# High and low parts of each row block side by side in SBUF, and FFN up chunks 1 to 3 and 23 in the wide two-part product

## The chip, the cores and the metric

The kernel runs on one core of one Trainium2 chip. The metric is device time in microseconds (us) of one execution; lower is better. Before the change the median of 3 runs is 851.08 us (850.93 to 851.29).

## What is computed

The reference chains two transformer-like blocks over 256 tokens of width 1024. Only one part of the first block matters here, its feed-forward network:

```python
h = rmsnorm(x, ffn_pre_norm[l])
up = causal_dwconv(h @ w_ffn_up[l], ffn_conv_w[l], ffn_conv_b[l])   # 1024 -> 6144, 3 taps over tokens
f_gate, f_val = jnp.split(up, 2, axis=-1)
f = (jax.nn.gelu(f_gate, approximate=True) * f_val) @ w_ffn_down[l] # 3072 -> 1024
x = x + rmsnorm(f, ffn_post_norm[l])
```

Everything is float32. The kernel reaches that precision on TensorE by splitting each operand into a high part, which TensorE takes in one pass (type fp32r), and a low part, the rest. A product is then three matmuls: high by high, weights high by rows low, and weights low by rows high.

## The kernel before

**Weights.** They come in as 258 units of 128 x 1024. For each unit SyncE starts a transfer, ScalarE copies it to the high part (L1359), VectorE subtracts to get the low part (L1942), and TensorE uses both. Four places hold split units, so ScalarE can split a unit only when TensorE is done with the unit four before it. The program of each engine is written out by hand; an engine works through its own list strictly in order, and semaphores tie the lists together.

**Rows.** The activations (8 blocks k of 128 channels by 256 tokens) are held as a high and a low part too: tile `HX` with views `Hh` and `Hl`, and tile `BR` with views `YBh` and `YBl`. In both, all eight high blocks stand first and all eight low blocks behind them.

**FFN up.** There are 24 chunks, fu0 to fu23, each of two units (one gives the gate channels, one the value channels). Per unit and block k there are two ways:

- `chunk` with `three`: three matmuls of 256 columns (L666, L667, L668), all summed in one half of a PSUM bank. Chunks fu1, fu2, fu3 and fu23 go this way; fu0 too, in another order (`chunk_by_k`).
- `chunk_apart` with `apart` (L719): the high weights meet high and low rows in one matmul of 512 columns, and the low weights meet the high rows in one of 256 columns, which is added to the second half of the bank. Each unit has a bank of its own, and VectorE sums the two halves with one reduction a unit (L2665) into `FSUM`. The list `APART` (L259), here fu4 to fu22, says which chunks go this way.

After a chunk come, in this order: (for `APART` the two reductions on VectorE), the convolution's first tap on ScalarE (two instructions, L1370), its other taps on VectorE (four instructions, L1963), gelu on ScalarE, the product of gate and value on VectorE (L1953), its high part on ScalarE (into `YBh`), its low part on GpSimd (L2757; for fu23 on VectorE). On VectorE the splits of two coming units and the product of the chunk before stand ahead of a chunk's reductions or taps.

**FFN down.** After each odd chunk from fu3 to fu21, two units of `fd` multiply finished products: `down_rows`, 12 matmuls a unit, 512 columns of weights moving past a stationary row block. The last four units stand behind fu23 in an order of (token half, unit) written out by hand, in which the product of chunk 23 (i = 3) comes fifth, as `(0, 3)`. Behind that follows `second_norm`, the norm of the sum over all chunks on ScalarE and VectorE, beside TensorE's memory values (mk2, mk3); the second block's first products (`vu`) need its result.

Two more lines are touched: unit `SPARE` (153) is split into `BR` while that is free, and `bank_table` gives each chunk its banks (for odd chunks in `APART` banks 2 and 0, for even ones 1 and 3).

Of the kernel before, what the change touches and what calls it, by code (L numbers as in the profile page):

```python
# [8 lines left out]
R = mybir.dt.float32r  # L9
# [7 lines left out]
P = 128  # L17
T = 256
# [237 lines left out]
    return {"g": name[:5], "u": name[:5], "w": name.split("_")[0], "m": "mv", "v": name[:2]}[name[0]]  # L256


APART = [f"fu{j}" for j in range(4, 23)]  # L259
SPARE = FIRST["mk2"] + 1  # L260


def place(q):

    return (q - (q > SPARE)) % NS
# [9 lines left out]
def bank_table():  # L275

    bank, n = {}, 1
    for name, _, _ in STREAM:
# [8 lines left out]
        elif name in ("mk0", "mk1"):  # L287
            bank[name] = 1 + int(name[2])
        elif name[:2] == "fu" and name in APART:
            for i in range(2):  # L290
# [66 lines left out]
def build_program(nc, first, gates, ws, par, con, masks, bd, rows, swt, xin, xtok, min_, post, decay, gates2, out):  # L357
    ctx = ExitStack()
    with ctx:
        def sb(name, shape, dt=F):  # L360
            return ctx.enter_context(nc.sbuf_tensor("t_" + name, shape, dt))
# [10 lines left out]
        PB = [ctx.enter_context(nc.psum_tensor(f"bank{i}", [P, 512], F)) for i in range(8)]  # L372
# [18 lines left out]
        BR = sb("br", [P, 2, 2048], R)  # L391

        def ar(kb, *shape):
            n = 1
            for k in shape:
                n *= k
            v = ARENA[:, kb * 256:kb * 256 + n]
            if len(shape) == 2:
                return v.rearrange("p (a b) -> p a b", a=shape[0])
            if len(shape) == 3:  # L400
                return v.rearrange("p (a b c) -> p a b c", a=shape[0], b=shape[1])
            return v
# [3 lines left out]
        WL = [sb(f"wl{i}", [P, 1024], R) for i in range(NS)]  # L406
# [3 lines left out]
            return BR[:, 0, 0:1024] if q == SPARE else WH[place(q)][:, :]  # L410

        def low(q):
            return BR[:, 1, 0:1024] if q == SPARE else WL[place(q)][:, :]

        HX = sb("hx", [P, 2, 8, T], R)
        Hh, Hl = HX[:, 0, :, :], HX[:, 1, :, :]
        SM = sb("sm", [P, 394])
        NW = SM[:, 304:352].rearrange("p (a b) -> p a b", a=3)
        NW2 = SM[:, 352:364].rearrange("p (a b) -> p a b", a=3)
# [26 lines left out]
        DTS = WH[NS - 1][:, 0:256].rearrange("p (k c) -> p k c", k=8)  # L446
        BAW = ar(60, 8, 8)
        BAS = BR[:, 0, 0:128].rearrange("p (k c) -> p k c", k=8)
        YBh, YBl = (BR[:, i, :].rearrange("p (k t) -> p k t", k=8) for i in range(2))
        MEMF, MEMQ = ar(16, 8, T), ar(24, 8, T)  # L450
        MG = ar(36, 8, T)
        MP = ar(44, 8, T)
# [47 lines left out]
        def half(bank, j):  # L500
            return PB[bank][:, T * j:T * j + T]

        def two(bank):
            return PB[bank][:, :].rearrange("p (k t) -> p k t", k=2)

        def ffn_source(name, i):

            return FSUM[:, 2 * (int(name[2:]) % 2) + i, :] if name in APART else half(BANK[name], i)

# [152 lines left out]
        def pe_program(e):  # L662
# [7 lines left out]
            def mm(o, l, r, st=True, sp=True):  # L670
                return e.matmul(o, l, r, start=st, stop=sp, skip_group_check=True)  # L671
# [4 lines left out]
            def weights(q, a):  # L676
                return [w.rearrange("p (a b) -> p a b", a=a) for w in (high(q), low(q))]
# [40 lines left out]

            def apart(b, wh, wl, k):  # L719

                mm(two(b), wh[:, k, :], HX[:, :, k, :], k == 0, False)
                return mm(half(b, 1), wl[:, k, :], Hh[:, k, :], False, k == 7)

            def chunk_apart(name):
                for j in range(2):
                    q = walk.unit()
                    wh, wl = weights(q, 8)
                    split_ready(q)
                    bank_free((name, j))
                    for k in range(8):  # L730
                        if k == 4:
                            walk.mid()
                        m = apart(BANK[name, j], wh, wl, k)
                    m.then_inc(*unit.now(q))
                    walk.tick()

            def chunk_by_k(name, xh, xl, x_ready):
                b = BANK[name]
                qs = [walk.unit(NS - 1 - j) for j in range(LAST[name] - FIRST[name] + 1)]
                for q in qs:  # L740
                    split_ready(q)
                bank_free(name)
                for k in range(8):
                    x_ready(k)
                    for j, q in enumerate(qs):
                        wh, wl = weights(q, 8)
                        m = three(half(b, j), wh[:, k, :], wl[:, k, :], xh[:, k, :], xl[:, k, :], k == 0 and j == 0, k == 7)
                        if k == 7:
                            m.then_inc(*unit.now(q))
# [421 lines left out]
            def normed(tag):  # L1171
                def ready(k):
                    e.wait_ge(*(g_hl if k % 2 and tag == "mix" else d_hl).of(tag, k))
                return ready
# [80 lines left out]
            for j in range(24):  # L1255
                if j == 0:
                    chunk_by_k("fu0", Hh, Hl, normed("fpre"))
                elif f"fu{j}" in APART:
                    chunk_apart(f"fu{j}")
# [94 lines left out]
        def act_program(e):  # L1354
# [441 lines left out]
            for j in range(24):  # L1796
                name = f"fu{j}"
                walk.cols(name, j == 0)
                e.wait_ge(*(d_ev.of(name) if name in APART else unit.of(LAST[name])))
                if j >= 2:  # L1800
# [138 lines left out]
        def dve_program(e):  # L1939
            def split(q):  # L1940
                e.wait_ge(*hi.of(q))
                e.tensor_tensor(low(q), RAW[q % NR][:, :], high(q).bitcast(F), SUB).then_inc(*lo.now(q))  # L1942
# [716 lines left out]
            for j in range(24):  # L2659
                name = f"fu{j}"  # L2660
                walk.cols(name, j == 0)
                if name in APART:
                    for i in range(2):
# [310 lines left out]
```

## Time and profile before

| what | value |
|---|---|
| median of 3 runs | 851.08 us (850.93 to 851.29) |
| profiled execution: span | 849.0 us |
| median less span (start and end around the profiled instructions) | 2.1 us |
| TensorE matmul busy | 836.9 us (99%) |
| VectorE busy | 650.2 us (77%) |
| ScalarE busy | 508.5 us (60%) |

The profiled execution's own time is not listed apart from its span; the 2.1 us are the median less the span. A matmul's row gives its start and its whole length through the array, and matmuls overlap in it, so what a matmul costs in a stream is the distance from its start to the next one's start, called its pitch here. The same holds, more weakly, for VectorE, where an instruction's last stretch overlaps the next.

### The profile page before, as it was taken

The numbers are of one execution on the slowest core, as the hardware profiler recorded it, in microseconds if no ns is written. First come the engines' busy times: TensorE is split into PE (matmuls) and PEld (weight loads), VectorE is DVE, ScalarE is ACT, GpSimd is POOL, SyncE is SP. The second block draws the span as 40 slices with busy tenths as digits, with TensorE's granted clock in tenths as the row PEclk, the third lists the DMA queues.
The fourth block names the chain that finished last, engine by engine and source line by source line (L and its number), as shares of the span: only waits on it lengthen the run. The fifth ranks groups of instructions, "written<-read, shape, count | busy, mean of one in ns | idle before, by whom it ended". The sixth has DMA issues, their size and how long they took to land. (4 is left out here: it accounts for less than half of the span.)

```text
span 849.0 us, 13946 instructions
## 1 busy us (share of the span) xinstructions
PE 836.9 (99%) x5422; PEld 755.0 (89%) x5422; DVE 650.2 (77%) x1171; ACT 508.5 (60%) x840; POOL 76.1 (9%) x76
## 2 busy tenths in 40 slices
PE   8999999999999999999999999999999999999996
PEld 7999999999989988888888799899899888888885
DVE  6887987998877877888777868778855566776764
ACT  6575778665377755565657878754553454545443
POOL 0100002001020211111111200140000020000000
PEclk9999999999999999999999999999999999999999
DMA  8657443467455655546555454644423332455541
GB/s 314 236 170 279 152 147 125 148 200 296 148 178 189 220 186 200 181 167 213 184 188 185 150 200 172 244 155 152 146 100 117 108 125 100 136 197 189 198 149 49
DMA packets 40729, 148.42 MB, mean 175 GB/s; under 512 B 4668, under 2 KB 5592, under 8 KB 40024
## 3 DMA queue, kind: packets, MB, share of 16 engines
q1 hardware_dynamic: 40520, 147.40, 50.6%
q8 instruction: 43, 0.70, 0.3%
q14 instruction: 22, 0.18, 0.1%
q10 hardware_dynamic: 144, 0.13, 0.0%
HBM read 146.44 MB, written 1.08 MB: 174 GB/s over the span
## 5 line engine op out<-in xcount | busy, mean ns | idle before, releaser
L1942 DVE TENSOR_TENSOR t_wl<-t_raw,t_wh 128x1024 fp32r<-128x1024 f32 x256 | 312.7, 1230 | 81.0 <-ACT t_wh L1359 80.0
L1359 ACT ACTIVATE t_wh<-t_raw 128x1024 fp32r<-128x1024 f32 x256 | 268.1, 1055 | 88.4 <-PE bank L671 49.1
L666 PE MATMUL bank<-t_hx,t_wh 128*128 128x256 f32 x832 | 241.9, 291 | 1.2 <-POOL t_hx L2757 0.7
L668 PE MATMUL bank<-t_hx,t_wl 128*128 128x256 f32 x832 | 235.3, 283 | 0.0
L667 PE MATMUL bank<-t_hx,t_wh 128*128 128x256 f32 x832 | 235.3, 283 | 0.0
L666 PEld LDWEIGHTS bank<-t_hx,t_wh 128*128 128x128 f32 x832 | 159.3, 191 | 3.8 <-issue 1.4
L667 PEld LDWEIGHTS bank<-t_hx,t_wh 128*128 128x128 f32 x832 | 159.4, 192 | 0.5
L668 PEld LDWEIGHTS bank<-t_hx,t_wl 128*128 128x128 f32 x832 | 159.3, 191 | 0.0
L671 PE MATMUL bank<-t_wh,t_hx 128*128 128x512 f32 x440 | 147.7, 401 | 1.4 <-DVE t_wl L1942 0.8
L671 PE MATMUL bank<-t_wh,t_br 128*128 128x512 f32 x384 | 123.6, 393 | 0.0
L671 PE MATMUL bank<-t_hx,t_wh 128*128 128x512 f32 x304 | 107.7, 398 | 0.0
L671 PEld LDWEIGHTS bank<-t_wh,t_hx 128*128 128x128 f32 x440 | 82.7, 188 | 18.6 <-DVE t_wl L1942 2.1
L671 PEld LDWEIGHTS bank<-t_wh,t_br 128*128 128x128 f32 x384 | 72.1, 188 | 15.4 <-issue 0.2
L671 PE MATMUL bank<-t_wl,t_hx 128*128 128x512 f32 x220 | 85.8, 390 | 0.0
L671 PE MATMUL bank<-t_hx,t_wl 128*128 128x256 f32 x304 | 85.3, 281 | 0.0
L671 PE MATMUL bank<-t_wl,t_br 128*128 128x512 f32 x192 | 74.9, 390 | 0.0
L1370 ACT ACTIVATE t_arena<-bank 128x512 f32<-128x512 f32 (+5 forms) x76 | 42.0, 573 | 53.7 <-PE bank L671 28.2
L671 PEld LDWEIGHTS bank<-t_hx,t_wh 128*128 128x128 f32 x304 | 57.1, 188 | 14.1
L2757 POOL TENSOR_TENSOR t_br<-t_arena,t_br 128x256 fp32r<-128x256 f32 x29 | 33.7, 1165 | 399.4 <-ACT t_br L1370 399.4
L671 PE MATMUL bank<-t_arena 128*128 128x128 f32 (+4 forms) x370 | 58.4, 305 | 1.2 <-DVE t_arena L2535 1.2
L671 PEld LDWEIGHTS bank<-t_hx,t_wl 128*128 128x128 f32 x304 | 57.4, 189 | 0.4
L1963 DVE SCALAR_TENSOR_TENSOR t_arena<-t_arena,t_par 128x255 f32<-128x255 f32 (+2 forms) x88 | 36.6, 479 | 24.8 <-ACT t_arena L1370 24.8
(159 smaller groups left out, 1001.8 us busy)
## 6 DMA issues: line engine op xcount, KB each, us to landing
t_raw<-in_ws SPq DMA_DIRECT2D x258, 512.0 KB, 4.0
t_br<-decay SPq DMA_DIRECT2D x1, 2048.0 KB, 8.8
t_arena<-in_post SPq DMA_DIRECT2D x3, 512.0 KB, 5.1
t_arena<-gates SPq DMA_DIRECT2D x1, 1536.0 KB, 10.6
t_x<-in_xin SPq DMA_DIRECT2D x2, 512.0 KB, 4.5
t_bd<-in_bd SPq DMA_DIRECT2D x1, 1024.0 KB, 6.8
t_x<-in_xtok SPq DMA_DIRECT2D x1, 1024.0 KB, 6.6
t_arena<-in_mem SPq DMA_DIRECT2D x1, 1024.0 KB, 8.7
```

The lines of the kernel that those rows point to most:

```text
L666: e.matmul(o, wh, xh, start=first, stop=False, skip_group_check=True)
L667: e.matmul(o, wh, xl, start=False, stop=False, skip_group_check=True)
L668: return e.matmul(o, wl, xh, start=False, stop=last, skip_group_check=True)
L671: return e.matmul(o, l, r, start=st, stop=sp, skip_group_check=True)
L1359: e.activation(high(q), RAW[q % NR][:, :], ACT.Copy, bias=0.0, scale=1.0).then_inc(*hi.now(q))
L1370: return e.activation(o, i, f, bias=bias, scale=scale)
L1942: e.tensor_tensor(low(q), RAW[q % NR][:, :], high(q).bitcast(F), SUB).then_inc(*lo.now(q))
L1963: return e.scalar_tensor_tensor(out=o, in0=a, scalar=s, in1=b, op0=op0, op1=op1)
L2757: return e.tensor_tensor(o, a, b, op)
```

## The change

`HX` and `BR` are laid out anew: for each block k its high part and its low part stand next to each other, so that 512 consecutive values of a partition are the high and low row block. The 512-column matmul of `apart` then reads one run of 512 where it read two runs of 256 that lay 2048 values apart, and writes the bank as one run. Every other use of `Hh`, `Hl`, `YBh`, `YBl` goes through the new views; those that take two blocks at once now read or write two runs of 256 where they had one of 512. The low part of the unit `SPARE` moves to where the high parts of blocks 2 and 3 and their low parts now stand. And `APART` becomes fu1 to fu23, so that chunks 1, 2, 3 and 23 take the wide product as well, with their two reductions each.

```diff
-APART = [f"fu{j}" for j in range(4, 23)]
+APART = [f"fu{j}" for j in range(1, 24)]
...
-            return BR[:, 1, 0:1024] if q == SPARE else WL[place(q)][:, :]
-
-        HX = sb("hx", [P, 2, 8, T], R)
-        Hh, Hl = HX[:, 0, :, :], HX[:, 1, :, :]
+            return BR[:, 0, 1024:2048] if q == SPARE else WL[place(q)][:, :]
+
+        HX = sb("hx", [P, 8, 2, T], R)
+        YB = BR.rearrange("p a b -> p (a b)").rearrange("p (k w t) -> p k w t", k=8, w=2)
+        Hh, Hl = HX[:, :, 0, :], HX[:, :, 1, :]
...
-        YBh, YBl = (BR[:, i, :].rearrange("p (k t) -> p k t", k=8) for i in range(2))
+        YBh, YBl = YB[:, :, 0, :], YB[:, :, 1, :]
...
-                mm(two(b), wh[:, k, :], HX[:, :, k, :], k == 0, False)
+                mm(PB[b][:, :], wh[:, k, :], HX[:, k, :, :].rearrange("p w t -> p (w t)"), k == 0, False)
```

## Rows read from the trace of the kernel before

**Rows 1.** The page: busy time (share) xinstructions, and the granted clock in 40 slices

```profile
PE 836.9 (99%) x5422; PEld 755.0 (89%) x5422; DVE 650.2 (77%) x1171; ACT 508.5 (60%) x840; POOL 76.1 (9%) x76
...
PEclk9999999999999999999999999999999999999999
```

**Rows 2.** Windows, one of the FFN: PE, PEld, DVE, ACT, POOL busy, clock, DMA

```profile
400.00:450.00 50.00, 50.00 (x264) 42.58 (x264) 40.29 (x60) 29.08 (x42) 6.93 (x6) 1.00 0.57 188
```

**Rows 3.** Timeline of PE in fu1, three matmuls a block: start, length

```profile
273.96 0.28 PE L666 MATMUL bank<-t_hx,t_wh 128*128 128x256 f32 x1
...
274.68 0.28 PE L666 MATMUL bank<-t_hx,t_wh 128*128 128x256 f32 x1
```

**Rows 4.** Timeline of PE in fu4: first four blocks' starts, and its second unit

```profile
296.70 0.39 PE L671 MATMUL bank<-t_hx,t_wh 128*128 128x512 f32 x1
296.93 0.28 PE L671 MATMUL bank<-t_hx,t_wl 128*128 128x256 f32 x1
297.04 0.40 PE L671 MATMUL bank<-t_hx,t_wh 128*128 128x512 f32 x1
...
298.10 0.40 PE L671 MATMUL bank<-t_hx,t_wh 128*128 128x512 f32 x1
...
299.51 0.40 PE L671 MATMUL bank<-t_hx,t_wh 128*128 128x512 f32 x1
```

**Rows 5.** Timeline of PE behind fu23: 512-column matmuls with one moving run

```profile
459.24 0.40 PE L671 MATMUL bank<-t_wh,t_br 128*128 128x512 f32 x1
...
459.71 0.62 PE L671 MATMUL bank<-t_wh,t_br 128*128 128x512 f32 x2
...
463.80 0.61 PE L671 MATMUL bank<-t_wh,t_br 128*128 128x512 f32 x2
```

**Rows 6.** Timeline of PE: 256 columns with 16 or 8 columns of weights

```profile
496.04 2.01 PE L671 MATMUL bank<-t_hx,t_br 128*16 128x256 f32 x16
```

**Rows 7.** Timeline of DVE from fu21's reductions on

```profile
443.00 1.28 DVE L2665 TENSOR_REDUCE t_arena<-bank 128x256 f32<-128x512 f32 x2
445.44 1.67 DVE L1963 SCALAR_TENSOR_TENSOR t_arena<-t_arena,t_par 128x255 f32<-128x255 f32 x4 [1.16 <-ACT t_arena L1370]
447.02 1.22 DVE L1942 TENSOR_TENSOR t_wl<-t_raw,t_wh 128x1024 fp32r<-128x1024 f32 x1
448.16 0.42 DVE L1953 TENSOR_TENSOR t_arena<-t_arena 128x256 f32<-128x256 f32 x1
448.50 1.22 DVE L1942 TENSOR_TENSOR t_wl<-t_raw,t_wh 128x1024 fp32r<-128x1024 f32 x1
```

**Rows 8.** Timeline of DVE behind fu1

```profile
279.78 1.23 DVE L1942 TENSOR_TENSOR t_wl<-t_raw,t_wh 128x1024 fp32r<-128x1024 f32 x1 [0.32 <-ACT t_wh L1359]
281.00 1.65 DVE L1963 SCALAR_TENSOR_TENSOR t_arena<-bank,t_par,t_arena 128x255 f32<-128x255 f32 x4
```

**Rows 9.** Timelines of ACT (first row) and DVE behind fu23

```profile
459.44 1.02 ACT L1370 ACTIVATE t_arena<-bank,t_par 128x256 f32<-128x256 f32 x2 [0.26 <-PE bank L668]
...
458.65 1.22 DVE L1942 TENSOR_TENSOR t_wl<-t_raw,t_wh 128x1024 fp32r<-128x1024 f32 x1
460.50 1.66 DVE L1963 SCALAR_TENSOR_TENSOR t_arena<-bank,t_par,t_arena 128x255 f32<-128x255 f32 x4 [0.64 <-ACT t_arena L1370]
...
464.11 0.42 DVE L1953 TENSOR_TENSOR t_br<-t_arena,t_br 128x256 fp32r<-128x256 f32 x1 [0.48 <-ACT t_br L1370]
```

**Rows 10.** The chain that ended last, behind fu23: start, length, what

```profile
462.16 1.13 DVE t_wl L1942
...
465.50 2.18 ACT t_hx L1370 x4
...
478.17 1.15 DVE t_wl L1942
...
479.36 1.66 PE bank L671 x6
...
```

**Rows 11.** Groups of DVE by form: xcount, busy us, mean ns of one

```profile
L2665 DVE TENSOR_REDUCE t_arena<-bank 128x256 f32<-128x512 f32 x38 | 24.3, 682 | 0.0
L1953 DVE TENSOR_TENSOR t_arena<-bank,t_arena 128x512 f32<-128x512 f32 x14 | 9.4, 684 | 3.8 <-ACT t_arena L1391 3.8
```

## The prediction

> **What bounds the kernel now.** I read the page first. TensorE is busy 99% of the span at the full granted clock of 2.4 GHz, VectorE 77%, ScalarE 60% [rows 1]. So a gain can only come from TensorE's own list, unless a change makes another engine late. The windows say the same of the FFN: in 50 us TensorE is busy for all 50, VectorE for 40 [rows 2]. Then I read TensorE's timeline for pitches, since the length of a matmul's row overlaps the next one. In fu1 six matmuls of 256 columns take from 273.96 to 274.68, so 120 ns each and 360 ns a block [rows 3]. In fu4 three blocks of one wide and one narrow matmul take from 297.04 to 298.10, so 353 ns a block, and the first block took 340 ns, from 296.70 to 297.04 [rows 4]. A 512-column matmul whose moving operand is one run has a pitch of 227 ns: 18 of them between 459.71 and 463.80 [rows 5]. Last I read VectorE's timeline (rows 7 to 9) and the chain that ended last: behind fu23 it leaves TensorE for some 17 us, runs on ScalarE and VectorE, and comes back to TensorE at 479.36 [rows 10]. That stretch decides this case beside the pitches.
>
> **The pitch of a wide pair.** What the change does for TensorE is to shorten the two-run matmul. No row shows 512 columns in one run taking turns with 256, so I bound it. Lower end: 340 ns, the first block of fu4 [rows 4]; it is also 227 [rows 5] plus 113, and with 16 or 8 columns of weights a 256-column matmul came down to (2.01 - 0.28) / 15 = 115 ns [rows 6]. Upper end: the 353 of today, the second run costing nothing. Between them lies 227 [rows 5] + 120 [rows 3] = 347 ns, two streams as they stand with 128 columns of weights, as this pair has; I take that. The saving against today is 353.3 - 347 = 6.3 ns a pair, between 0 and 13.3.
>
> The Trainium skill, in "Advanced Engine Details and Errata", section SBUF Cachelines, says that SBUF is read in 16-byte lines and that the penalty falls on accesses that change the line each time. Two runs of 1 KB have one break among 128 lines, so by that rule the new layout saves next to nothing, and the sum below would be that of the first rival. Rows 4 agree in that the first two-run matmul of fu4 is followed after 0.23 us, like one in a single run; the blocks behind it do not agree.
>
> **fu4 to fu22.** These are 19 chunks of two units of eight blocks, 304 pairs. All count from fu4's second unit on, 37 units or 296 pairs: 296 x 6.3 ns = 1.9 us less on TensorE (0 to 3.9). Why fu4's first unit doesn't count comes next.
>
> **fu1 to fu3.** TensorE's own saving is 48 blocks x (360 - 347) = 0.6 us. But each chunk puts two reductions on VectorE, which take 1.28 us together [rows 7], and ScalarE's first tap has to wait for them. What stands behind each is known from fu21: reductions at 443.00, taps at 445.44 (they wait 1.16 us for ScalarE), the next split at 447.02, the product at 448.16, a second split at 448.50 that holds VectorE for 1.14 us, as the first one does. So one turn takes 449.64 - 443.00 = 6.64 us [rows 7]. TensorE's chunk without a down step takes 16 x 347 ns = 5.55 us. VectorE falls behind by 1.1 us a chunk. Its turn begins at 281.00, where the taps of fu1 begin today, right behind a split [rows 8]. Then fu2's reductions start at 287.64, fu3's at 294.28, and the split behind fu3's taps, that of fu4's second unit, at 294.28 + 4.02 = 298.30; it lands 1.22 us later, at 299.52. TensorE would be ready for it at 273.96 + 6 units x 2.78 + 2 down units x 12 x 0.227 + 2.78 = 298.9. Today it starts there at 299.51 [rows 4]. So the waiting split gives all of TensorE's 0.6 us back, and fu4's second unit starts when it does today. Behind the waiting reductions are queued exactly these splits; behind ScalarE's first tap its own splits and the gelu. I take 0, with 0.3 us to either side, since the turn was read in another stretch. The down step behind fu3 has only two splits on VectorE, and a pair of chunks with its down step leaves VectorE 20% idle [rows 2], so I let the lag die out within the next pairs.
>
> **fu23.** TensorE saves 16 x 13 ns = 0.2 us, and the chunk's evacuation gets longer. Today ScalarE takes the first tap at 459.44, right behind TensorE, and VectorE the others at 460.50 [rows 9]. VectorE's split before that starts at 458.65 and holds the engine for 1.14 us, so the reductions start at 459.79 and the taps 2.44 us later [rows 7], at 462.23: 1.73 us later than today. All the rest follows in order: gelu, product, its low part (464.11 today [rows 9]), which the fifth down step waits for. TensorE has four steps of six matmuls before that, until 459.24 + 4 x 1.36 = 464.68 [rows 5], and the low part lands at 464.53: a cover of 0.15 us. TensorE will wait there. That wait alone could be made up later, but the same ScalarE list goes on to the row copies at 465.50, and VectorE's to a split that lands at 479.32, which TensorE waits for at 479.36 [rows 10]. No step of that chain waits for anything else today. So 1.73 us reach the end in full, and fu23's 0.2 us are inside that wait. It all happens earlier by what fu4 to fu22 saved, since each turn of VectorE there starts from a unit that TensorE has finished.
>
> **The rest of the layout.** Some 40 instructions on ScalarE, VectorE and GpSimd take two blocks at once and now have two runs. A reduction that reads pairs of values 256 apart takes 682 ns, a contiguous operation on as many values from PSUM 684 [rows 11], so I price these at nothing. Only the four row copies at 465.50 are on the chain; a tenth more on each would be 0.2 us. Matmuls of 256 columns and the down and token products read single runs as before. SPARE moves within space that is free at the same time. No transfer is added or moved; SyncE's and GpSimd's lists stay as they are.
>
> **The sum.** 0 (fu1 to fu4) - 1.9 (fu4 to fu22) + 1.7 (tail) = -0.2 us on the span of 849.0, so 848.8; the 2.1 us around the span stay, which makes 850.9 for the median of 851.08. Every nanosecond of the pair moves it by 0.3 us, and the break-even is a pair of 353.3 - 5.8 = 347.5 ns: this is a change of two effects that nearly cancel.
>
> **The rivals.**
>
> First, on the slower side: the second run costs nothing, and the pair stays at 353 because wide and narrow matmuls take turns. Then only the tail is left, +1.7 us, 852.8. It decides from a pair above 347.5 ns. For it speaks that the first wide matmul shows no loss though it has two runs; against it, that today's pair is dearer than its two parts in streams of their own (353 against 347).
>
> Second: the pair falls to 340. Then 296 x 13.3 ns = 3.9 us are saved, and 3.9 - 1.7 = 2.2 us are left: 848.9. For it speak the first block at 340 and the 115 ns of narrow weights; against it, that a full 128 columns of weights go with 120 in every stream of 256 [rows 3].
>
> Third: the tail is hidden after all, if ScalarE's or VectorE's list has slack that the rows don't show. Then 1.9 us and fu23's 0.2 are left: 849.0. Against it speaks the chain, which has hardly a gap there [rows 10].
>
> Fourth: VectorE's lag from fu1 to fu3 doesn't die out at once, and a second wait of up to 1 us comes in the next chunks: 851.9.
>
> That the change doesn't do what it says can only mean the first rival: that 64 matmuls go and 8 reductions come is plain from the code.
>
> **How the numbers follow.** About 1.7 us (0.2%) is what a measurement here can tell from no change. I give the forecast 45% (pairs of 344 to 349 ns, 850.0 to 851.6), the first rival 25%, the second 20%, the third 4%, the fourth 6%. Faster by over 0.2% (under 849.4) are the second and third rival and a little of the forecast: 22%. Slower by over 0.2% (over 852.8) is half of the first rival and part of the fourth: 16%. Within: 62%. The range that holds 8 in 10 reaches to both outer cases, from 848.8 to 852.9. The forecast's own range is 850.0 to 851.6.
>
> **What would show it.** In TensorE's timeline of fu5 or later: three pairs in 1.04 us if I am right, 1.06 by the first rival, 1.02 by the second. At fu4's second unit: a start near 299.5 and a TensorE wait of about 0.6 us for a split. Behind fu23: a wait of 1.5 to 1.9 us before the fifth down step, and taps that follow the end of fu23 by some 3 us where it is 1.3 today. My prediction is wrong if the wide pair is far from 347, or if the chain behind fu23 keeps its length from fu23's end to the first product behind it.

## The result, and the profile after

The changed kernel is slower: 852.62 us (median of 15 runs, 852.41 to 852.94) against 851.03 us (15 runs, 850.64 to 851.39) for the kernel before beside it. The ratio is 1.002, with a 95% interval of 1.0013 to 1.0027. The profiled span is 850.6 us where it was 849.0. The prediction was 0.2 us less than before; the measurement is 1.6 us more. The time lies outside the forecast's own range of 850.0 to 851.6, inside the range of 8 in 10 (848.8 to 852.9), and near the first rival's 852.8.

The page of the changed kernel, its busy times and granted clock, answers [rows 1]:

```profile
PE 836.4 (98%) x5358; PEld 751.2 (88%) x5358; DVE 654.2 (77%) x1179; ACT 508.3 (60%) x840; POOL 76.0 (9%) x76
...
PEclk9999999999999999999999999999999999999999
```

TensorE has 64 matmuls less and only 0.5 us less busy time, at the same clock. A span that grows by 1.6 us with a busy time that shrinks means waits. The same FFN window as [rows 2] shows an unchanged steady state, with TensorE busy for all 50 us:

```profile
400.00:450.00 50.00, 50.00 (x264) 42.58 (x263) 40.26 (x61) 29.06 (x42) 6.99 (x6) 1.00 0.59 188
```

TensorE's timeline of the changed kernel, first at the start of fu4 and at its second unit, answering [rows 4], then in a later chunk (columns: start, length):

```profile
296.27 0.39 PE L672 MATMUL bank<-t_hx,t_wh 128*128 128x512 f32 x1
...
296.61 0.40 PE L672 MATMUL bank<-t_hx,t_wh 128*128 128x512 f32 x1
...
296.96 0.40 PE L672 MATMUL bank<-t_hx,t_wh 128*128 128x512 f32 x1
...
298.96 0.28 PE L672 MATMUL bank<-t_hx,t_wl 128*128 128x256 f32 x1
299.38 0.51 PE L672 MATMUL bank<-t_hx,t_wh 128*128 128x512 f32 x1
...
316.23 0.40 PE L672 MATMUL bank<-t_hx,t_wh 128*128 128x512 f32 x1
...
317.29 0.40 PE L672 MATMUL bank<-t_hx,t_wh 128*128 128x512 f32 x1
```

Three pairs take 317.29 - 316.23 = 1.06 us, 353 ns each. That is the pitch of before, although the wide matmul now reads and writes one run. The first pair of fu4 again takes 340 ns and the next one 350. At 299.38 a start comes 0.42 us after the narrow matmul ahead of it, where 0.12 is usual: a wait of 0.3 us at fu4's second unit.

VectorE's timeline behind fu1, fu2 and fu3 (first four rows, answering [rows 8]) and behind fu23 (the rest, answering [rows 9]); the bracket is the idle time before the group and what ended it:

```profile
280.81 1.28 DVE L2666 TENSOR_REDUCE t_arena<-bank 128x256 f32<-128x512 f32 x2
...
287.45 1.28 DVE L2666 TENSOR_REDUCE t_arena<-bank 128x256 f32<-128x512 f32 x2
...
294.08 1.28 DVE L2666 TENSOR_REDUCE t_arena<-bank 128x256 f32<-128x512 f32 x2
...
298.11 1.22 DVE L1943 TENSOR_TENSOR t_wl<-t_raw,t_wh 128x1024 fp32r<-128x1024 f32 x1
...
459.71 1.28 DVE L2666 TENSOR_REDUCE t_arena<-bank 128x256 f32<-128x512 f32 x2
462.15 1.67 DVE L1964 SCALAR_TENSOR_TENSOR t_arena<-t_arena,t_par 128x255 f32<-128x255 f32 x4 [1.16 <-ACT t_arena L1371]
465.77 0.42 DVE L1954 TENSOR_TENSOR t_br<-t_arena,t_br 128x256 fp32r<-128x256 f32 x1 [0.48 <-ACT t_br L1371]
```

The reductions behind fu1 to fu3 come 6.64 and 6.63 us apart, longer than TensorE's chunk, and the split that fu4's second unit waits for starts at 298.11. Behind fu23 the taps start 462.15 - 460.50 = 1.65 us later than in [rows 9]. ScalarE's first tap, which was released by TensorE there, is now released by the reduction:

```profile
461.02 1.09 ACT L1371 ACTIVATE t_arena<-t_arena,t_par 128x256 f32<-128x256 f32 x2 [1.92 <-DVE t_arena L2666]
```

TensorE's timeline behind fu23 has the first down step, right behind fu23, and the wait itself at the fifth:

```profile
459.06 0.40 PE L672 MATMUL bank<-t_wh,t_br 128*128 128x512 f32 x1
...
466.35 0.47 PE L672 MATMUL bank<-t_wh,t_br 128*128 128x512 f32 x1 [1.63 <-DVE t_br L1954]
```

The same four points of the chain that ended last as in [rows 10]:

```profile
463.82 1.14 DVE t_wl L1943
...
467.17 2.18 ACT t_hx L1371 x4
...
479.84 1.14 DVE t_wl L1943
...
481.03 1.66 PE bank L672 x6
```

They lie 1.66, 1.67, 1.67 and 1.67 us later than in [rows 10]. So the delay arises between fu23 and the first of these points, and nothing behind it takes any of it back. TensorE comes to the end of fu23 only 0.2 us earlier than before (459.06, where [rows 5] have 459.24), and 0.12 of that is there already at fu1's start (273.84, where [rows 3] have 273.96). The forecast had it come 2.1 us earlier, 1.9 from fu4 to fu22 and 0.2 in fu23: the expected gain is not there.

### The profile page after: what moved, and what is told of

The parts are those of the page before. It is cut to its first block and busy times, and to the rows that moved or that the text cites. A ratio compares the mean times of both kernels' runs of the same rounds, so it can differ in the third digit from the quotient of the medians.

```text
span 850.6 us, 13830 instructions
## 1 busy us (share of the span) xinstructions
PE 836.4 (98%) x5358; PEld 751.2 (88%) x5358; DVE 654.2 (77%) x1179; ACT 508.3 (60%) x840; POOL 76.0 (9%) x76
## 5 line engine op out<-in xcount | busy, mean ns | idle before, releaser
L667 PE MATMUL bank<-t_hx,t_wh 128*128 128x256 f32 x768 | 223.7, 291 | 1.2 <-POOL t_hx L2758 0.7
L668 PE MATMUL bank<-t_hx,t_wh 128*128 128x256 f32 x768 | 217.1, 283 | 0.0
L667 PEld LDWEIGHTS bank<-t_hx,t_wh 128*128 128x128 f32 x768 | 147.0, 191 | 3.7 <-issue 1.4
L668 PEld LDWEIGHTS bank<-t_hx,t_wh 128*128 128x128 f32 x768 | 147.1, 192 | 0.5
L672 PE MATMUL bank<-t_hx,t_wh 128*128 128x512 f32 x368 | 130.5, 399 | 0.1
L672 PEld LDWEIGHTS bank<-t_hx,t_wh 128*128 128x128 f32 x368 | 69.1, 188 | 17.5 <-DVE t_wl L1943 0.5
L1964 DVE SCALAR_TENSOR_TENSOR t_arena<-t_arena,t_par 128x255 f32<-128x255 f32 (+2 forms) x104 | 43.3, 479 | 29.4 <-ACT t_arena L1371 29.4
L1371 ACT ACTIVATE t_arena<-t_arena,t_par 128x256 f32<-128x256 f32 x50 | 27.4, 594 | 55.6 <-DVE t_arena L2666 50.9
```

The lines of the kernel that those rows point to most:

```text
L667: e.matmul(o, wh, xh, start=first, stop=False, skip_group_check=True)
L668: e.matmul(o, wh, xl, start=False, stop=False, skip_group_check=True)
L1371: return e.activation(o, i, f, bias=bias, scale=scale)
L1964: return e.scalar_tensor_tensor(out=o, in0=a, scalar=s, in1=b, op0=op0, op1=op1)
```

## The experiments

My theory after the result: the tail costs its 1.7 us as worked out, and the pitch of the wide pair, not its layout, is where the step failed. Each experiment is given with the median of the kernel before beside it on the same chip. The kernels with fu4 to fu22 alone have no reductions on the tail and none behind fu1 to fu3.

### One part of the change at a time

The new layout alone, made from the changed kernel:

```diff
-APART = [f"fu{j}" for j in range(1, 24)]
+APART = [f"fu{j}" for j in range(4, 23)]
```

> The new layout alone, chunks 4 to 22 wide as before. Theory: the layout changes nothing, three wide pairs of fu5 take 1.06 us as before and the median is that of before, 851.0 (within 0.4 us). Rival: the layout does cost or save something elsewhere (two-run instructions on ScalarE, VectorE and GpSimd), which the changed kernel hides: then it is off by 0.5 us or more.

851.01 us against 850.99, a ratio of 0.9999 (0.999 to 1.0007). TensorE's timeline has three pairs in 1.06 us:

```profile
316.00 0.40 PE L672 MATMUL bank<-t_hx,t_wh 128*128 128x512 f32 x1
...
317.06 0.40 PE L672 MATMUL bank<-t_hx,t_wh 128*128 128x512 f32 x1
```

The layout alone does nothing that the medians or the pitch show: the second run of the moving operand had cost nothing. In the bank there was nothing to gain: the two runs that the old matmul wrote stood end to end (`two` is a view of the whole bank).

The other half, the four chunks in the old layout, made from the kernel before:

```diff
-APART = [f"fu{j}" for j in range(4, 23)]
+APART = [f"fu{j}" for j in range(1, 24)]
```

> The old layout with chunks 1 to 23 wide. Theory: the list of chunks alone makes the loss, so 852.6 as in the changed kernel, with a wait of about 1.8 us on TensorE behind fu23. Rival (the layout has a part in it): 0.5 us or more off 852.6.

852.80 us against 850.99, 1.0019 (1.001 to 1.0028), which can't be told from the changed kernel, with the same wait of 1.63 us before the fifth down step. So the whole loss is in the choice of chunks. The next two split it: chunks 1 to 22, and 4 to 23, both in the new layout.

```diff
-APART = [f"fu{j}" for j in range(1, 24)]
+APART = [f"fu{j}" for j in range(1, 23)]
```

> The changed kernel with chunk 23 by three matmuls a block, as before. Theory: the loss is chunk 23's reductions on the tail, so it goes: 850.9, fu4's second unit starting 0.1 us earlier than before and all behind it moved by that. Rival: VectorE's lag from fu1 to fu3 is what costs, and 23 little: 852.0 or more.

851.11 us against 850.99, 0.9998 (0.9989 to 1.0006). Neither loss nor gain is left; 850.9 was expected. On TensorE's timeline the wait at fu4's second unit has stayed (this start comes 0.43 us after the narrow matmul ahead of it), and the fifth down step starts without one:

```profile
299.35 0.28 PE L672 MATMUL bank<-t_hx,t_wl 128*128 128x256 f32 x1
299.78 0.51 PE L672 MATMUL bank<-t_hx,t_wh 128*128 128x512 f32 x1 [0.15 <-DVE t_wl L1943]
...
464.81 0.67 PE L672 MATMUL bank<-t_wh,t_br 128*128 128x512 f32 x2
465.32 0.39 PE L672 MATMUL bank<-t_wl,t_br 128*128 128x512 f32 x1
```

```diff
-APART = [f"fu{j}" for j in range(1, 24)]
+APART = [f"fu{j}" for j in range(4, 24)]
```

> The changed kernel with chunks 1 to 3 by three matmuls, 23 wide. Theory: the tail's 1.7 us are there in full: 852.7, with a wait of about 1.8 us in TensorE's list behind fu23. Rival (the lag from fu1 to fu3 costs): 851.2 or less.

852.71 us against 850.99, 1.002 (1.0011 to 1.0029), with the same wait as in the changed kernel:

```profile
466.32 0.47 PE L672 MATMUL bank<-t_wh,t_br 128*128 128x512 f32 x1 [1.63 <-DVE t_br L1954]
```

Chunk 23 alone makes the whole loss of 1.7 us. Chunks 1 to 3 make no difference that can be told, in either direction.

### What keeps the pair at 353 ns

If turns and not runs make the pair dear, longer stretches of one kind should make it cheaper, in both layouts. The eight wide matmuls of a unit first and then its eight narrow ones (by eights), with fu4 to fu22, in the new layout. `wide` and `narrow` are the two matmuls of `apart`, now a function each, which the code below doesn't show:

```diff
-APART = [f"fu{j}" for j in range(1, 24)]
+APART = [f"fu{j}" for j in range(4, 23)]
...
-                        m = apart(BANK[name, j], wh, wl, k)
+                        wide(b, wh, k)
+                    for k in range(8):
+                        m = narrow(b, wl, k)
```

> New layout, chunks 4 to 22 wide, and in each unit all eight wide matmuls first, then the eight narrow ones: the same 16 matmuls in another order. Theory A: the pair costs 353 ns because wide and narrow take turns; in streams of their own they cost 227 and 120, so a unit falls from 2.82 to 2.78 us and 304 pairs x 6 ns give 849.2. Theory B: 353 is what these columns cost in any order: a unit stays at 2.82 us and the time at 851.0.

849.25 us against 850.98, 0.9979 (0.9971 to 0.9988). The timeline of TensorE, one unit:

```profile
302.63 2.00 PE L672 MATMUL bank<-t_hx,t_wh 128*128 128x512 f32 x8
304.47 1.11 PE L672 MATMUL bank<-t_hx,t_wl 128*128 128x256 f32 x8
305.42 0.40 PE L672 MATMUL bank<-t_hx,t_wh 128*128 128x512 f32 x1
```

A unit takes 305.42 - 302.63 = 2.79 us, 349 ns a pair, where eight pairs of 353 take 2.82. The eight wide ones take 1.84 us (230 ns each), the eight narrow ones 0.95 (119). The same edit in the old layout, made from the kernel before, so that `wide` is its matmul of two runs:

```diff
...
-                        m = apart(BANK[name, j], wh, wl, k)
+                        wide(b, wh, k)
+                    for k in range(8):
+                        m = narrow(b, wl, k)
```

> The old layout, chunks 4 to 22, the eight wide matmuls first, then the eight narrow ones. Theory A with the layout of no effect: 849.2 as with the new layout. If the second run of a wide matmul costs something that taking turns had hidden, the wide ones have a pitch over 227 ns here and the time lies between 849.2 and 851.0.

849.27 us against 850.98, 0.9979 (0.997 to 0.9988). Its eight wide matmuls, of two runs each, take 304.12 - 302.27 = 1.85 us:

```profile
302.27 2.00 PE L671 MATMUL bank<-t_hx,t_wh 128*128 128x512 f32 x8
304.12 0.40 PE L671 MATMUL bank<-t_hx,t_wl 128*128 128x256 f32 x2
```

One run or two makes no difference in this order either. The gain of 1.7 us comes from the order alone. How short may the stretches be? Two wide, then two narrow (by twos), in the new layout:

```diff
-APART = [f"fu{j}" for j in range(1, 24)]
+APART = [f"fu{j}" for j in range(4, 23)]
...
-                    for k in range(8):
+                    for k in range(0, 8, 2):
...
-                        m = apart(BANK[name, j], wh, wl, k)
+                        wide(b, wh, k)
+                        wide(b, wh, k + 1)
+                        narrow(b, wl, k)
+                        m = narrow(b, wl, k + 1)
```

> New layout, chunks 4 to 22, two wide matmuls, then two narrow ones, and so on: half as many turns. Theory A: half of the 6 ns a pair: 850.1, two pairs in 0.70 us. Theory B: 851.0.

849.19 us against 850.98, 0.9979 (0.997 to 0.9987), with four pairs in 304.62 - 303.22 = 1.40 us:

```profile
303.22 0.63 PE L672 MATMUL bank<-t_hx,t_wh 128*128 128x512 f32 x2
...
304.62 0.40 PE L672 MATMUL bank<-t_hx,t_wh 128*128 128x512 f32 x1
```

Twos do as well as eights, where half of the gain was expected (850.1). A single unit, in rows rounded to 10 ns, is too short to weigh 6 ns a pair. From fu5's start to fu23's there are 288 pairs and nine down steps. The first two rows are these two starts in the kernel before, the third is fu23's start by eights (fu5 starts at 302.63, above), and the last two are both starts by twos:

```profile
302.34 0.40 PE L671 MATMUL bank<-t_hx,t_wh 128*128 128x512 f32 x1
...
453.48 0.28 PE L666 MATMUL bank<-t_hx,t_wh 128*128 128x256 f32 x1
...
452.15 0.28 PE L667 MATMUL bank<-t_hx,t_wh 128*128 128x256 f32 x1
...
302.53 0.40 PE L672 MATMUL bank<-t_hx,t_wh 128*128 128x512 f32 x1
...
451.81 0.28 PE L667 MATMUL bank<-t_hx,t_wh 128*128 128x256 f32 x1
```

That is 151.14 us in turns, 149.52 by eights and 149.28 by twos: 5.6 and 6.5 ns less a pair. Not all of it lies in the pairs. A unit takes 2.82 us on average in turns, 2.79 by eights and 2.78 by twos, so 353, 348 and 348 ns a pair; a down step behind them takes 5.50, 5.47 and 5.45 us.

So the price is not one of each change of length alone: a unit by eights goes from wide to narrow and back once, by twos four times, in turns eight times, and twos cost no more than eights. What else turns over with each matmul? Two candidates were tried, both made from the changed kernel with the list set back to fu4 to fu22 as above and with strict turns. First the place that the narrow product is added to, so that it goes to the first half of the bank:

```diff
-                return mm(half(b, 1), wl[:, k, :], Hh[:, k, :], False, k == 7)
+                return mm(half(b, 0), wl[:, k, :], Hh[:, k, :], False, k == 7)
```

> New layout, chunks 4 to 22, wide and narrow matmuls in turns, the narrow one added to the first half of the bank in place of the second; VectorE sums the halves, so the result is the same. Theory P: taking turns costs because the narrow matmul adds to the half that the wide one has just written; then the pair falls below 353 ns (three in under 1.05 us) and the time below 850.4. Theory Q: it is not the half: 353 ns and 851.0.

851.04 us against 850.95, 1.0001 (0.9992 to 1.001). Three pairs still take 1.06 us:

```profile
315.98 0.40 PE L672 MATMUL bank<-t_hx,t_wh 128*128 128x512 f32 x1
...
317.04 0.40 PE L672 MATMUL bank<-t_hx,t_wh 128*128 128x512 f32 x1
```

Then the weights, so that the narrow product takes its weights from the tile that the wide one has just used:

```diff
-                return mm(half(b, 1), wl[:, k, :], Hh[:, k, :], False, k == 7)
+                return mm(half(b, 1), wh[:, k, :], Hh[:, k, :], False, k == 7)
```

> New layout, chunks 4 to 22, in turns, the narrow matmul loading the high weights once more in place of the low ones: the share of the low weights is left out. Theory W: taking turns costs because the two weight loads of a pair come from two tiles; then the pair falls towards 347 ns and the time to 849.2 to 850.0. Theory Q: it is the alternation of 512 and 256 columns itself: 353 ns and 851.0.

851.09 us against 850.95, 1.0001 (0.9992 to 1.001). Neither is the cause.

Nor do turns always have this price. In the kernel with the four chunks in the old layout, TensorE waits at fu4's second unit as it does in the changed kernel, and fu5 behind it runs in strict turns at another pitch, from its first matmul to the down step behind it:

```profile
302.71 0.39 PE L671 MATMUL bank<-t_hx,t_wh 128*128 128x512 f32 x1
...
308.25 0.39 PE L671 MATMUL bank<-t_wh,t_br 128*128 128x512 f32 x1
```

Its 16 pairs take 308.25 - 302.71 = 5.54 us, 346 ns each, about the 347 of the prediction. From fu6 on a pair takes 353 on average again. In the changed kernel fu5 takes 5.66 us behind the same kind of wait; that kernel has the new layout, but the kernel before has the old one and the dear pitch too. So the same order, half, weight tiles and rows run at either price. What decides between them, and why turns mostly run at the dear one, stays open.

### Is the sum right once the pitch is?

The changed kernel, chunks 1 to 23, with eight wide and then eight narrow:

```diff
...
-                        m = apart(BANK[name, j], wh, wl, k)
+                        wide(b, wh, k)
+                    for k in range(8):
+                        m = narrow(b, wl, k)
```

> The changed kernel, chunks 1 to 23, with the eight wide matmuls of a unit ahead of its eight narrow ones. If the prediction failed in the pitch of the pair alone, its sum comes out once the pair has the pitch that it took: 852.6 less 296 pairs x 4 to 6 ns (1.2 to 1.8 us), so 850.8 to 851.4, with the wait behind fu23 still there. Rival: the sum failed in another step too, and the time is 850.3 or less, or 851.9 or more.

851.21 us against 850.95, 1.0004 (0.9995 to 1.0013). Here the pair has almost the pitch that the prediction gave it, and the time is nearly the one predicted: what fu4 to fu22 gain, the tail takes back. TensorE's timeline has both waits, at fu4's second unit and at the fifth down step:

```profile
299.58 2.11 PE L672 MATMUL bank<-t_hx,t_wh 128*128 128x512 f32 x8 [0.40 <-DVE t_wl L1949]
...
464.97 0.47 PE L672 MATMUL bank<-t_wh,t_br 128*128 128x512 f32 x1 [1.76 <-DVE t_br L1960]
```

### A version that beats both

Chunk 23 goes back to three products, which leaves the tail as it was. Chunks 1 to 3 keep the wide product, but the wait at fu4's second unit is moved: wide matmuls need the high part of the weights alone, so only they are put behind its wait, and the wait for the low part, VectorE's split, comes ahead of the narrow ones.

```diff
-APART = [f"fu{j}" for j in range(1, 24)]
+APART = [f"fu{j}" for j in range(1, 23)]
...
-                    split_ready(q)
+                    e.wait_ge(*hi.of(q))
                     bank_free((name, j))
                     for k in range(8):
...
-                        m = apart(BANK[name, j], wh, wl, k)
+                        wide(b, wh, k)
+                    split_ready(q)
+                    for k in range(8):
+                        m = narrow(b, wl, k)
```

> New layout, chunks 1 to 22 wide, eight wide matmuls first behind a wait for the high part alone, the low part being waited for only ahead of the eight narrow ones; chunk 23 by three. Theory A: TensorE then waits less for VectorE's lag at fu4, since the low part is due 1.8 us later, so up to 0.6 us from fu1 to fu3 come on top of the 1.9 us: 848.6. Theory B (353 in any order): 850.6.

848.73 us against 850.98, 0.9972 (0.9961 to 0.9983). On TensorE's timeline fu4's second unit starts at 299.19, 0.95 us after the eight narrow ones ahead of it, so without a wait, and its narrow matmuls follow the eight wide ones after 1.85 us, without one too:

```profile
298.24 1.12 PE L672 MATMUL bank<-t_hx,t_wl 128*128 128x256 f32 x8
299.19 2.00 PE L672 MATMUL bank<-t_hx,t_wh 128*128 128x512 f32 x8
301.04 1.11 PE L672 MATMUL bank<-t_hx,t_wl 128*128 128x256 f32 x8
```

That is 0.5 us less than the same order with fu4 to fu22 (849.25): what TensorE saves in fu1 to fu3, now kept. The start of fu1, first in the kernel with chunks 1 to 23 by eights just above and then in this one, tells the effect of the later wait from that of the chunks:

```profile
274.03 0.40 PE L672 MATMUL bank<-t_hx,t_wh 128*128 128x512 f32 x1
...
274.20 0.40 PE L672 MATMUL bank<-t_hx,t_wh 128*128 128x512 f32 x1
```

From there to fu4's second unit it takes 299.58 - 274.03 = 25.55 us with the old wait, as long as in the kernel before (299.51 - 273.96 in [rows 3] and [rows 4]), and 299.19 - 274.20 = 24.99 us with the later one. From that unit to the end of fu23 this kernel and the one with fu4 to fu22 by eights take the same 158.1 us. By twos with the same two waits and the same list, the low part's wait ahead of the first narrow matmul:

```diff
...
-                    split_ready(q)
+                    e.wait_ge(*hi.of(q))
                     bank_free((name, j))
-                    for k in range(8):
+                    for k in range(0, 8, 2):
...
-                        m = apart(BANK[name, j], wh, wl, k)
+                        wide(b, wh, k)
+                        wide(b, wh, k + 1)
+                        if k == 0:
+                            split_ready(q)
+                        narrow(b, wl, k)
+                        m = narrow(b, wl, k + 1)
```

> New layout, chunks 1 to 22 wide, two wide and two narrow matmuls in turns, the first two wide ones behind a wait for the high part alone, the low part being waited for ahead of the first narrow one. If the two gains add (1.8 us by twos, 0.5 us from chunks 1 to 3 with the later wait): 848.6, as with eight and eight. If the low part is needed too early again, since only 0.46 us of wide matmuls stand ahead of it where 1.8 us stood: a wait of some tenths at fu4's second unit and 849.0 or more.

848.67 us against 851.06, 0.9974 (0.9964 to 0.9983), the same as by eights. Two wide matmuls cover less of the late split, so some of the wait is back on TensorE's timeline: the first two pairs of fu4's second unit take 300.12 - 299.20 = 0.92 us where two pairs take 0.70.

```profile
299.20 0.63 PE L672 MATMUL bank<-t_hx,t_wh 128*128 128x512 f32 x2
299.78 0.50 PE L672 MATMUL bank<-t_hx,t_wl 128*128 128x256 f32 x2
300.12 0.63 PE L672 MATMUL bank<-t_hx,t_wh 128*128 128x512 f32 x2
```

Both versions stand 2.3 to 2.4 us below the kernel before.

## Why the prediction was wrong

**The step that failed is the pitch of the wide pair.** I took 347 ns, the sum of two streams; it stayed at 353. At 296 pairs that is the whole forecast gain of 1.9 us. With a gain of zero, the prediction's own sum gives 0 - 0 + 1.7, the first rival's 852.8, against 852.62 measured. The first rival was right in its price, and in that the second run costs nothing (the layout alone, 851.01 against 850.99; eight wide matmuls in 1.84 us with one run, 1.85 with two). Its reason, the turns, holds in part: by twos or by eights the time is 849.2, but fu5 of the four chunks in the old layout took 346 ns a pair in turns, so turns alone don't make the 353, and what does is open.

How the reading went wrong: 353 against 347 was seen, and put down to the one feature that the change removes. The two differ in two features, runs and turns. The streams of [rows 3] and [rows 5] have neither two runs nor turns, so the 6 ns could be either's, and no row of before separated them. The one row that did bear on it was the first pair of fu4, whose two-run matmul was followed after 0.23 us [rows 4]; I gave it a quarter of the weight. The rule of the Trainium skill, "Advanced Engine Details and Errata", section SBUF Cachelines, pointed the same way: by it, a break once in 128 lines should cost next to nothing. The runs agree with it (851.01 against 850.99). I wrote that the blocks behind the first pair did not agree. They did: the same 353 stands there without the second run.

**The estimate of 347 itself was fair, for another order.** By eights and by twos a pair takes 348 ns on average. By eights the changed kernel measures 851.21, against the 850.9 predicted, inside the forecast's own range.

**fu1 to fu3 were right in their result.** The turn of VectorE was 6.64 us as taken from fu21, the reductions start at 280.81, 287.45 and 294.08 (predicted 281.00, 287.64 and 294.28, on a trace in which fu1 starts 0.12 us later), and the split at 298.11 (298.30). fu4's second unit starts at 299.38 (about 299.5). TensorE's wait there is 0.3 us and not 0.6, since TensorE itself came later with pairs of 353. Nothing is left of its saving: 851.11 with chunks 1 to 22. That the lag dies out was right too: from fu4's second unit to the end of fu23 it takes 459.06 - 299.38 = 159.68 us, where it took 459.24 - 299.51 = 159.73. So the fourth rival is out.

**The tail was right.** Taps at 462.15 (462.23), 1.65 us later than before (1.73); a TensorE wait of 1.63 us (1.5 to 1.9) before the fifth down step; taps 3.1 us after the end of fu23 (some 3); the chain 1.67 us later up to 481.03, nothing of it made up. Chunk 23 alone gives 1.7 us. The third rival, hidden slack, is out.

**The rest of the layout at nothing was right.** The layout alone takes 851.01 us against 850.99. VectorE's busy time rises by 4.0 us [rows 1], less than the 5.1 us of the eight new reductions; the four row copies on the chain take 2.18 us as before [rows 10], with two runs instead of one. The groups of VectorE's reductions by form answer [rows 11]:

```profile
L2666 DVE TENSOR_REDUCE t_arena<-bank 128x256 f32<-128x512 f32 x46 | 29.4, 680 | 0.0
```

**The second rival** (340 ns, for all pairs) was not seen in any order. The 340 belong to the first pair behind a down step, not to fu4 alone: every even chunk from fu4 to fu22 begins with it, before and after. In fu6 of the kernel before it takes 313.84 - 313.50 = 0.34 us:

```profile
313.50 0.39 PE L671 MATMUL bank<-t_hx,t_wh 128*128 128x512 f32 x1
...
313.84 0.40 PE L671 MATMUL bank<-t_hx,t_wh 128*128 128x512 f32 x1
```

**One sum among the chances was off:** 22% for a gain of over 0.2% is less than the 20 and 4% of the two rivals that it is made of.

## What to carry to other kernels

Where a stream is dearer than its parts and differs from them in two features, a change that removes one of them can't be credited with the difference; look for a row that has only one, or price both cases. Work added to the evacuation of the last piece before a serial stretch counts in full, while the same work behind an earlier piece can vanish: here two reductions cost 1.7 us behind fu23, and those behind fu1 to fu3 no more than TensorE's small saving there. Where a product needs only part of what it waits for, put the part that doesn't need it first: 0.5 us here, where it let three more chunks keep what they save.

## What was not expected of the hardware

A matmul of 512 columns and one of 256, in strict turns, take 353 ns a pair on average; two and two or eight and eight take 348, at the same clock, and the down steps behind them are shorter too (5.45 and 5.47 us, where 5.50 follow turns). By the medians that is 851.0 against 849.2 us, for 304 pairs. Whether the operand is one run or two, which half of the bank the narrow one adds to and which weight tile it loads made no difference. In one stretch, fu5 behind a wait, the same turns took 346 ns a pair. What the price depends on beside the order was not found.
